# Fourier mixing folded over the positions, x2 stored before its scale, the context norm spread over gate b

## The chip, the cores and the metric

The kernel runs on one core of a Trainium2 chip. A core has five engines that work side by side: TensorE (PE, matrix products into the accumulators called PSUM), VectorE (DVE), ScalarE (ACT), GpSimd (POOL, here mostly an issuer of transfers) and SyncE (SP, an issuer of transfers). The metric is the device time of one execution in microseconds. The kernel before takes 2562.43 us, the median of 3 runs (2561.29 to 2563.51).

## The reference

Two transformer blocks stand one behind the other, over 1024 positions of 1024 channels: the first has sliding-window attention and a squared-ReLU MLP, then `rms_norm(h, final_norm)`; the second has a modulated norm, latent attention, a Fourier branch, two sigmoid gates and 16 experts. The change lies in the Fourier branch, in gate b, and where x enters the merge:

```python
def _fourier(f):                       # f: (B, T=1024, 512), in 4 groups of 128 channels
    fg = f.reshape(B, T, 4, 128).astype(jnp.float32)
    y = jnp.fft.fft2(fg, axes=(1, 3), norm="ortho").real
    return y.reshape(B, T, 512)

h  = _modulate(_rms(x, norm1_g), sh1, sc1);   hc = _modulate(_rms(ctx, norm1_g), csh1, csc1)
p  = h @ w_in
gb = sigmoid(p[..., OFF_GB:N_IN])
x  = x + g1 * ((ga * (attn_o @ w_o_attn) + gb * (_fourier(p[..., OFF_F:OFF_GA]) @ w_fourier)) @ w_out)
```

The real part of the two-dimensional transform is cos(positions) times cos(channels) minus sin(positions) times sin(channels). Cosine is even and sine odd about position 512, and each is again even or odd about 256; the change rests on this.

## The kernel before

Data lie channel by partition, 1024 positions along a row. Every product is done three times (`mm3`: high by high, low by high, high by low part of each operand), so every operand is split beforehand: ScalarE writes the high part (`make_hi` for weights, ACTIVATE Copy for data) and VectorE the rest (`make_lo`, a subtraction). Weights come through a ring of 3 raw buffers (SP issues their loads) and 4 places for split tiles; `tile(...)` numbers them in the order of use, and `done` says which product frees a place. PSUM has 8 banks of 512 columns; `next_banks` hands them out in rotation as the program is written, `claim` makes PE wait until the bank's last reader is through (`hand_over`). The order of the work on each engine is the order of the code, stage after stage: ..., MLP, final_*, four_*, gates_b_*, latent_*, heads_*, attention, merge_*, router_*, experts.

The stages that the change touches:
- final_*: the sums of squares (L1197), the two rows of factors spread over all partitions by a product with ones (L1205; row 0 for the second block's norm, row 1 for x's own scale in banks `f_rb1`), and U, the normed and modulated input, made tile k by tile k (DVE L1252, ACT L1218, DVE L1256).
- four_*: `f` = w_f times U for 4 groups (PE; groups 0 and 1 together as U's tiles come, 2 and 3 later), split into fT (ACT L1313, DVE L1335); the channel transform of each group, 8 blocks of 128 positions by 256 columns (cosine and sine) into Z (ACT L1317, DVE L1344); then the position transform: 16 tiles of a 2048 by 1024 table, each against 4 groups and both halves, into all 8 banks; then Y (ACT L1323, DVE L1351). In the middle, behind group 0's fT, DVE scales x into x2 (L1340, 8 instructions), and POOL stores it to memory (L1302); ACT's writing of Z over X waits for these stores.
- gates_b_*: for j = 0 to 7 gate b (48 products into 2 banks), a sigmoid (ACT L1458), w_fourier times Y (24 products), their product (DVE L1483) to memory. At j = 1 stands the context's norm as one piece: squares (ACT L269) and additions (DVE L275), sums (PE L283), root, diagonal, row (PE L310), and HC (DVE L1472 and L1475, ACT L1451).
- latent_*: among others the gate a products `ga_pe` and three rows of factors (L310).
- merge_*: POOL loads x2 (L2368), then gates and Fourier products (L2376, L2379); DVE makes M (L2403, L2407, L2409), PE multiplies by w_out, and DVE adds into X (L2416).

Of the kernel before, what the change touches and what calls it, by code (L numbers as in the profile page):

```python
# [102 lines left out]
def _program(nc, A, out, ctx):  # L103
# [1074 lines left out]
    fs_b, f_rb, f_rb1 = next_banks(), next_banks(2), next_banks(2)  # L1178
    fn.pe.plan(("sums",), ("row", 0), ("row", 1))
    fn.act.plan(("sd", 1), ("sd", 2), *[("hi", k) for k in range(8)])  # L1180
# [10 lines left out]
    def final_pe(pe):  # L1191
# [76 lines left out]
    f_b = {(g, i): next_banks(1, (f_rb, f_rb + 1, f_rb1, f_rb1 + 1)) for g in range(2) for i in range(2)}  # L1268
    z_b = {}
    for g in range(4):  # L1270
        if g > 1:
            for i in range(2):
                f_b[g, i] = next_banks(1, (f_rb1, f_rb1 + 1))
        for n in range(4):
            z_b[g, n] = next_banks(1, (f_rb1, f_rb1 + 1) if g == 0 else ())
    fo.act.plan(("cd",))
    fo.dve.plan(("cd",))
    for g in range(4):
        fo.act.plan(*[("f", g, i) for i in range(2)], *[("z", g, n) for n in range(4)])
# [4 lines left out]
    fo.pe.plan(("f", 0), ("f", 1), *[("z", 0, n) for n in range(4)], *[("z", 1, n) for n in range(4)])
    for g in (2, 3):
        fo.pe.plan(("f", g, 0), ("f", g, 1), *[("z", g, n) for n in range(4)])
    fo.pe.plan(*[("dft", c) for c in range(16)])
    fo.act.plan(*[("y", g, i) for g in range(4) for i in range(2)])
    fo.dve.plan(*[("y", g, i) for g in range(4) for i in range(2)])
    turn[0] = 0  # L1290
    T_F = [tile("w_f", g, fo.pe("f", g) if g < 2 else fo.pe("f", g, 1)) for g in range(4)]
# [12 lines left out]
    def four_act(act):
        act.wait_ge(*cd_in.at(1))
        act.e.activation(cd[0][:], cdr[:], ACT.Copy).then_inc(*fo.act.one("cd"))
        for g in range(4):
            make_hi(act, T_F[g if g > 1 else 0] + 3)
            for i in range(2):
                act.wait_ge(*f_mark(g, i))  # L1310
                if g:
                    act.wait_ge(*fo.pe("z", g - 1, 3))
                act.e.activation(fT[0][:, half(i)], bank(f_b[g, i]), ACT.Copy).then_inc(*fo.act.one("f", g, i))  # L1313
            for n in range(4):
                act.wait_ge(*fo.pe("z", g, n))
# [1672 lines left out]
```

## Time and profile before

| | |
|---|---|
| median of 3 runs | 2562.43 us |
| the profiled execution's own time | 2562.86 us |
| its span | 2561.0 us |
| mean granted clock of PE | 0.959 |
| PE busy | 2339.9 us (91%) |
| DVE busy | 1465.0 us (57%) |
| ACT busy | 1033.8 us (40%) |
| POOL busy | 271.4 us (11%) |
| memory traffic | 112 GB/s over the span |

The span is what the profile's records cover; 1.86 us of the execution lie around it. All times in rows are microseconds from the span's start. A busy PE is not a full PE: a product's record is longer (0.39 us) than the distance to the next one, and that distance is what counts.

### The profile page before, as it was taken

What the parts mean: (1) busy time and instruction counts of PE and PEld (TensorE: products, weight loads), DVE (VectorE), ACT (ScalarE), POOL (GpSimd) and SP (SyncE); (2) the same over time, 40 slices, a digit from 0 to 9 for tenths busy, and PEclk for the clock granted to TensorE, in tenths of its full rate; (3) what the DMA queues carried; (4) which work ended last, traced back from release to release, by engine and by line L of the source; (5) the groups of instructions that cost most, each with busy time, mean ns of one, the idle gap of its engine ahead of it and who ended that gap; (6) DMA issues with size and microseconds to landing.
All of it is one profiled execution on the core that took longest, in us unless ns stands there. A gap on an engine that the chain in (4) does not pass through costs nothing.

```text
span 2561.0 us, 28342 instructions
## 1 busy us (share of the span) xinstructions
PE 2339.9 (91%) x11580; PEld 1937.3 (76%) x11580; DVE 1465.0 (57%) x2132; ACT 1033.8 (40%) x1570; POOL 271.4 (11%) x360
## 2 busy tenths in 40 slices
PE   5999989999999999979999999899998988289997
PEld 3898768888888888758778878677777765268886
DVE  5677435454445445672232235867777543969997
ACT  3677324112212211432221123466666312258875
POOL 2111000011001111000000002700000100111211
PEclk9999999999999999989999999999999988689999
DMA  3124411243234333122222111100000621779996
GB/s 124 50 67 133 164 50 50 70 132 111 95 98 132 108 102 111 46 93 70 87 71 85 40 48 50 46 1 1 1 1 1 239 71 47 298 237 377 382 387 217
DMA packets 81026, 287.55 MB, mean 112 GB/s; under 512 B 10048, under 2 KB 10176, under 8 KB 79232
## 3 DMA queue, kind: packets, MB, share of 16 engines
q1 hardware_dynamic: 50256, 180.12, 19.6%
q0 software_dynamic: 29488, 101.43, 12.5%
q10 hardware_dynamic: 1152, 4.19, 0.4%
q8 instruction: 91, 1.49, 0.2%
q14 instruction: 39, 0.32, 0.0%
HBM read 250.05 MB, written 35.65 MB: 112 GB/s over the span
## 4 chain that ended last, share of the span: by engine, by line
PE 75%; DVE 14%; ACT 7%; DMA 1%; issue 1%; POOL 1%; POOLq 0%; DVEq 0%; ACTq 0%
PE psum L98 23%; PE psum L100 23%; PE psum L99 23%; DVE small L2268 4%; ACT PB L2204 3%; DVE MP_lo L2305 2%; ACT MP_hi L2234 1%; PE psum L868 1%; PE psum L841 1%; DVE idx L2545 1%; DVE vals L2543 1%; DVE cur L2548 1%; PE psum L310 1%; PE psum L2563 1%; DMA gal<-gas 1%
## 5 line engine op out<-in xcount | busy, mean ns | idle before, releaser
L98 PE MATMUL psum<-U_hi,w_hi 128*128 128x512 f32 (+1 forms) x1216 | 482.2, 397 | 20.7 <-DVE w_lo L231 9.3
L99 PE MATMUL psum<-U_lo,w_hi 128*128 128x512 f32 (+1 forms) x1216 | 479.1, 394 | 0.0
L100 PE MATMUL psum<-U_hi,w_lo 128*128 128x512 f32 (+1 forms) x1216 | 478.8, 394 | 0.0
L222 ACT ACTIVATE w_hi<-raw 128x1024 fp32r<-128x1024 f32 (+3 forms) x177 | 177.2, 1007 | 378.2 <-PE psum L100 370.0
L231 DVE TENSOR_TENSOR w_lo<-raw,w_hi 128x1024 fp32r<-128x1024 f32 (+3 forms) x177 | 206.2, 1172 | 190.4 <-ACT w_hi L222 190.1
L98 PEld LDWEIGHTS psum<-U_hi,w_hi 128*128 128x128 f32 (+1 forms) x1216 | 230.8, 190 | 74.2 <-issue 16.3
L100 PEld LDWEIGHTS psum<-U_hi,w_lo 128*128 128x128 f32 (+1 forms) x1216 | 230.0, 189 | 51.0 <-issue 0.8
L99 PEld LDWEIGHTS psum<-U_lo,w_hi 128*128 128x128 f32 (+1 forms) x1216 | 230.7, 190 | 48.1 <-issue 0.8
L98 PE MATMUL psum<-a_hi,w_hi 128*128 128x512 f32 x512 | 199.2, 389 | 0.0
L99 PE MATMUL psum<-a_lo,w_hi 128*128 128x512 f32 x512 | 199.2, 389 | 0.0
L100 PE MATMUL psum<-a_hi,w_lo 128*128 128x512 f32 x512 | 199.2, 389 | 0.0
L1058 DVE CUSTOM_DVE_ANT_0 mraw<-mraw,srow 128x512 f32<-128x512 f32 x128 | 85.8, 690 | 136.8 <-DMA mraw<-in_w_mod 130.2
L2305 DVE TENSOR_TENSOR MP_lo<-psum,MP_hi 128x512 fp32r<-128x512 f32 x160 | 109.6, 686 | 83.9 <-ACT MP_hi L2234 83.4
L1123 DVE TENSOR_TENSOR X<-psum,X 128x512 f32<-128x512 f32 x128 | 84.5, 688 | 96.6 <-PE psum L100 96.6
L1044 POOL DMA_DIRECT2D mraw<-in_w_mod x128 | 68.7, 537 | 657.7 <-DVE modb L1058 382.7
L231 DVE TENSOR_TENSOR w_lo<-rawe,w_hi 128x1024 fp32r<-128x1024 f32 x112 | 131.5, 1220 | 11.4 <-ACT w_hi L222 10.9
L1081 ACT ACTIVATE relu<-psum 128x512 f32<-128x512 f32 x64 | 38.2, 597 | 222.3 <-PE psum L100 217.5
L222 ACT ACTIVATE w_hi<-rawe 128x1024 fp32r<-128x1024 f32 x112 | 116.3, 1058 | 25.1 <-PE psum L100 25.1
L2140 PE MATMUL psum<-ident,PB 128*128 128x128 f32 x640 | 101.7, 282 | 23.4 <-DVE MP_lo L2305 22.2
L2140 PEld LDWEIGHTS psum<-ident,PB 128*128 128x128 f32 x640 | 75.7, 143 | 50.8 <-DVE MP_lo L2305 33.2
L2234 ACT ACTIVATE MP_hi<-psum 128x512 fp32r<-128x512 f32 x160 | 95.0, 594 | 42.5 <-PE psum L2140 41.5
L100 PEld LDWEIGHTS psum<-a_hi,w_lo 128*128 128x128 f32 x512 | 96.1, 188 | 20.0
(356 smaller groups left out, 4871.8 us busy)
## 6 DMA issues: line engine op xcount, KB each, us to landing
rawe<-in_w_e SPq DMA_DIRECT2D x112, 512.0 KB, 14.0
mraw<-in_w_mod POOLq DMA_DIRECT2D x128, 256.0 KB, 2.9
rawx<-in_w_e SPq DMA_DIRECT2D x56, 512.0 KB, 15.4
raw<-in_w_up SPq DMA_DIRECT2D x32, 512.0 KB, 3.6
raw<-in_w_dn SPq DMA_DIRECT2D x32, 512.0 KB, 3.6
raw<-in_w_e SPq DMA_DIRECT2D x24, 512.0 KB, 14.6
raw<-in_dft_t SPq DMA_DIRECT2D x16, 512.0 KB, 3.6
X<-in_xT SPq DMA_DIRECT2D x4, 1024.0 KB, 9.3
```

What stands on the lines that cost most here:

```text
L98: e.matmul(o, l[0], r[0], start=first, stop=False, skip_group_check=skip)
L99: e.matmul(o, l[0], r[1], start=False, stop=False, skip_group_check=skip)
L100: return e.matmul(o, l[1], r[0], start=False, stop=last, skip_group_check=skip)
L222: act.e.activation(w_hl[x.place][0][:, 0:x.width], w_raw[x.slot][:, 0:x.width], ACT.Copy).then_inc(w_hi, 1)
L231: dve.e.tensor_tensor(lo[:, 0:x.width], w_raw[x.slot][:, 0:x.width], f(hi[:, 0:x.width]), ALU.subtract).then_inc(w_lo, 1)
L1058: dve.e.tensor_tensor_reduce(mraw[n % 2][:], mraw[n % 2][:], srow[:, half(i % 2)], 1.0, 0.0, ALU.mult, ALU.add, dst).then_inc(*ml.dve.one( ...
L1123: dve.e.tensor_tensor(X[:, n, half(h)], bank(dn_b[i, n, h]), X[:, n, half(h)], ALU.add).then_inc(*ml.dve.one("x", i, n, h))
L2140: m = pe.e.transpose(bank(t_bank("turn", n), 256 * kb + P * i, 256 * kb + P * i + P), PB[(2 * u + i) % 5][:, (2 * t + kb) * P:(2 * t + kb ...
L2204: act.e.activation(PB[m % 5][:], s_of(m), ACT.Exp, bias=nmx[:, m % 8:m % 8 + 1], accum_out=msum(c)[:, z:z + 1]).then_inc(*at_s.act.one("ex ...
L2234: act.e.activation(MP[n % 4][0][:], bank(t_bank("turn", n)), ACT.Copy).then_inc(*at_s.act.one("turn", n))
L2268: dve.e.tensor_reduce(nmx[:, m % 8:m % 8 + 1], s_of(m), AX.X, ALU.max, negate=True).then_inc(*at_s.dve.one("max", m))
L2305: dve.e.tensor_tensor(lo[:], bank(t_bank("turn", n)), f(hi[:]), ALU.subtract).then_inc(*at_s.dve.one("turn", n))
```

## The change

The position transform is folded twice. After `f` (all 1024 positions of a group in two banks), ACT copies the second half out of PSUM (`second`), DVE forms the sums and differences f[n] +- f[1024-n], and then the same once more about 256 (`fold`); FF holds four quarters of 256 columns. The channel transform needs only cosine for the even half and only sine for the odd half, so its products are 128 columns wide (`over_channels`); one small float32 product with 3 columns gives what the fold leaves out (positions 256 and 512), and ACT's `alt` adds up the alternating sums for it. The position transform (`over_positions`) is 8 triples of products 256 columns wide for each group, with 2 table tiles in place of 16, and DVE unfolds its four parts into every second or fourth column of Y's row (`y`), some of them backwards. The groups run one after another in banks 4-5, 6-7, 2-3 and 0-1.

x is stored to memory without its scale as soon as the MLP has finished each tile; ACT copies the scale's row (`r1o`) and POOL stores it too. The 8 scaling instructions of DVE now stand in the merge (`x1`), behind a load of that row (`r1b`), which is issued ahead of the gates' loads. The context norm in gate b is spread: squares and additions at j = 1, sums at j = 2, row and HC at j = 4.

On PE, at the end of the channel transform and the start of the position transform, the rows before are (Z is stationary, w is a table tile):

```order
L99 MATMUL psum<-cd_lo,fT_hi 128x256
L100 MATMUL psum<-cd_hi,fT_lo 128x256
L98 MATMUL psum<-w_hi,Z_hi 128x512 [waits w_lo_made,fourier_dve]
L99 MATMUL psum<-w_lo,Z_hi 128x512
L100 MATMUL psum<-w_hi,Z_lo 128x512
```

After the change, at the end of group 0's position transform and the start of group 2's channel transform (L1486 is the 3-column product):

```order
L98 MATMUL psum<-w_hi,Z_hi 128x256
L99 MATMUL psum<-w_lo,Z_hi 128x256
L100 MATMUL psum<-w_hi,Z_lo 128x256
L1486 MATMUL psum<-small,cdr 128x3 [waits fourier_act,fourier_dve]
L98 MATMUL psum<-cd_hi,FF_hi 128x128 [waits fourier_dve]
L99 MATMUL psum<-cd_lo,FF_hi 128x128
L100 MATMUL psum<-cd_hi,FF_lo 128x128
```

One transform over 512 columns for all groups at the end has become a narrow one for each group, between the channel transforms.

On DVE, behind the last low part of U, before (cd is the channel table, X the scaling):

```order
L1330 TENSOR_TENSOR cd_lo<-cdr,cd_hi 128x256 [waits fourier_act]
L231 TENSOR_TENSOR w_lo<-raw_60,w_hi 128x1024 [waits w_hi_made]
L1335 TENSOR_TENSOR fT_lo<-psum,fT_hi 128x512 [waits fourier_act] x2
L1340 SCALAR_TENSOR_TENSOR X<-X,vec,psum 128x1024 [waits final_norm_products]
L1340 SCALAR_TENSOR_TENSOR X<-X,vec,psum 128x1024 x7
L1344 TENSOR_TENSOR Z_lo<-psum,Z_hi 128x512 [waits fourier_act] x4
```

and after, one `fold` (ff is the folded row; fe and fo the even and odd part):

```order
L1404 TENSOR_TENSOR ff_128<-psum,f2nd 128x1 [waits fourier_act]
L1405 TENSOR_TENSOR ff_128<-psum,f2nd 128x1
L1408 TENSOR_TENSOR fe<-psum,f2nd 128x511
L1409 TENSOR_TENSOR fo<-psum,f2nd 128x511
L1411 COPY small<-fe 128x1 [waits fourier_dve]
L1412 TENSOR_TENSOR ff_128<-fe 128x255
L1413 TENSOR_TENSOR ff_128<-fe 128x255
L1415 COPY ff_128<-fo 128x1 [waits fourier_dve]
L1416 TENSOR_TENSOR ff_128<-fo 128x255
L1417 TENSOR_TENSOR ff_128<-fo 128x255
```

The eight scalings have left this place, and ten short instructions for each group have come.

On POOL, at the start of the merge, the loads before are:

```order
L2368 DMA X<-x1s 128x2048 [waits x1_out0,attn_dve]
L2368 DMA X<-x1s 128x2048 [waits x1_out1]
L2368 DMA X<-x1s 128x2048 [waits x1_out2]
L2368 DMA X<-x1s 128x2048 [waits x1_out3]
L2376 DMA gal_202<-gas 128x1024 [waits ga_out2,ga_out0,ga_out3,ts_out1,ts_out0]
```

and after:

```order
L2520 DMA X<-x1s 128x2048 [waits x1_out0,attn_dve]
L2520 DMA X<-x1s 128x2048 [waits x1_out1]
L2520 DMA X<-x1s 128x2048 [waits x1_out2]
L2520 DMA X<-x1s 128x2048 [waits x1_out3]
L2522 DMA r1b<-r1s 128x1024 [waits r1_out]
L2530 DMA gal_215<-gas 128x1024 [waits ga_out2,ga_out0,ga_out3,ts_out1,ts_out0]
```

The row's load stands ahead of the first gate's.

```diff
@@ final norm @@
-    fs_b, f_rb, f_rb1 = next_banks(), next_banks(2), next_banks(2)
+    g_b = [4, 6, 2, 0]
+    fs_b, f_rb, f_rb1 = g_b[0], g_b[3], g_b[2]
+            if k == 3:
+                act.wait_ge(*fn.pe("row", 1))
+                act.e.activation(r1o[:], two(f_rb1), ACT.Copy).then_inc(*fn.act.one("r1o"))
@@ four_pool: x2 and the row of rsqrt to memory @@
+            pool.wait_ge(*ml.dve("x", 7, k, 1))
+            pool.e.dma_start(A["x1s"][:, k, :], X[:, k, :]).then_inc(x1_out[k // 2].sem, 16)
+        pool.wait_ge(*fn.act("r1o"))
+        pool.e.dma_start(A["r1s"], r1o[:]).then_inc(r1_out.sem, 16)
@@ four_act @@
+        def second(g):
+            act.wait_ge(*f_mark(g))
+            if g:
+                act.wait_ge(*fo.dve("fo", g - 1))
+            else:
+                act.wait_ge(*r1_out.at(1))
+            act.e.activation(f2nd[:], bank(g_b[g] + 1), ACT.Copy).then_inc(*fo.act.one("second", g))
+
+        def hi(g):
+            act.wait_ge(*fo.dve("fold", g))
+            if g > 1:
+                act.wait_ge(*fo.pe("chan", g - 2))
+            act.e.activation(FF[g % 2][0][:], ff[g % 2][:], ACT.Copy).then_inc(*fo.act.one("hi", g))
+            for s in range(2):
+                if g:
+                    act.wait_ge(*fo.act("alt", g - 1, s))
+                act.e.activation(alt[s][:], ff[g % 2][:, s:256:2], ACT.Copy, scale=(1.0, -1.0)[s],
+                                 accum_out=gx[:, 3 * g + 1 + s:3 * g + 2 + s]).then_inc(*fo.act.one("alt", g, s))
+
+        def one(g):
+            act.wait_ge(*fo.pe("e", g))
+            act.e.activation(ex[:, 3 * g:3 * g + 3], psum[:, g_b[g] + 1, 0:3], ACT.Copy,
+                             accum_out=y512[:, g:g + 1]).then_inc(*fo.act.one("e", g))
+
+        def z(g):
+            act.wait_ge(*fo.pe("chan", g))
+            if g > 1:
+                act.wait_ge(*fo.pe("pos", g - 2))
+            act.e.activation(Z[g % 2][0][:], two(g_b[g]), ACT.Copy).then_inc(*fo.act.one("z", g))
+
+        def second_p(g):
+            act.wait_ge(*fo.pe("pos", g))
+            if g:
+                act.wait_ge(*fo.dve("y", g - 1))
+            act.e.activation(p2nd[:], bank(g_b[g] + 1), ACT.Copy).then_inc(*fo.act.one("p2", g))
...
@@ four_dve @@
+        def fold(g):
+            x, a, b = ff[g % 2], bank(g_b[g]), f2nd
+            dve.wait_ge(*fo.act("second", g))
+            if g > 1:
+                dve.wait_ge(*fo.act("alt", g - 2, 1))
+                dve.wait_ge(*fo.dve("lo", g - 2))
+            e.tensor_tensor(x[:, 0:1], a[:, 0:1], b[:, 0:1], ALU.add)
+            e.tensor_tensor(x[:, 256:257], a[:, 0:1], b[:, 0:1], ALU.subtract)
+            if g:
+                dve.wait_ge(*fo.dve("fold", g - 1))
+            e.tensor_tensor(fe[:, 1:512], a[:, 1:512], b[:, 511:0:-1], ALU.add).then_inc(*fo.dve.one("fe", g))
+            e.tensor_tensor(fo_[:, 1:512], a[:, 1:512], b[:, 511:0:-1], ALU.subtract).then_inc(*fo.dve.one("fo", g))
+            dve.wait_ge(*fo.dve("fe", g))
+            e.tensor_copy(gx[:, 3 * g:3 * g + 1], fe[:, 256:257])
+            e.tensor_tensor(x[:, 1:256], fe[:, 1:256], fe[:, 511:256:-1], ALU.add)
+            e.tensor_tensor(x[:, 257:512], fe[:, 1:256], fe[:, 511:256:-1], ALU.subtract)
+            dve.wait_ge(*fo.dve("fo", g))
+            e.tensor_copy(x[:, 768:769], fo_[:, 256:257])
+            e.tensor_tensor(x[:, 513:768], fo_[:, 1:256], fo_[:, 511:256:-1], ALU.subtract)
+            e.tensor_tensor(x[:, 769:1024], fo_[:, 1:256], fo_[:, 511:256:-1], ALU.add).then_inc(
+                *fo.dve.one("fold", g))
...
+        def y(g):
+            a, b, x, E = bank(g_b[g]), p2nd, Yr[g % 2], ex[:, 3 * g:3 * g + 1]
+            dve.wait_ge(*fo.act("alt", 2 + g % 2, 1))
+            dve.wait_ge(*fo.dve("lo", 2 + g % 2))
+            if g > 1:
+                dve.wait_ge(*fo.dve("ylo", g - 2))
+            dve.wait_ge(*fo.act("e", g))
+            dve.wait_ge(*fo.act("p2", g))
+            e.tensor_copy(x[:, 512:513], y512[:, g:g + 1])
+            e.scalar_tensor_tensor(x[:, 0:512:4], a[:, 0:256:2], E, b[:, 0:256:2], ALU.add, ALU.subtract)
+            e.scalar_tensor_tensor(x[:, 1020:515:-4], a[:, 2:256:2], E, b[:, 2:256:2], ALU.add, ALU.add)
+            e.scalar_tensor_tensor(x[:, 2:512:4], a[:, 1:256:2], E, b[:, 1:256:2], ALU.subtract, ALU.subtract)
+            e.scalar_tensor_tensor(x[:, 1022:513:-4], a[:, 1:256:2], E, b[:, 1:256:2], ALU.subtract, ALU.add)
+            e.tensor_tensor(x[:, 1:512:2], a[:, 256:512], b[:, 256:512], ALU.subtract)
+            e.tensor_tensor(x[:, 1023:512:-2], a[:, 256:512], b[:, 256:512], ALU.add).then_inc(*fo.dve.one("y", g))
...
@@ four_pe (its 16 steps over the DFT tiles are gone) @@
-        for c in range(16):
-            w = use(pe, T_DFT[c])
-            for g in range(4):
-                l = [z[:, g, c % 8, 128 * (c // 8):128 * (c // 8) + 128] for z in (Zh, Zl)]
-                for i in range(2):
-                    m = mm3(pe.e, bank(2 * g + i), l, [x[:, half(i)] for x in w], c == 0, c == 15)
+        def over_channels(g):
+            x = FF[g % 2]
+            pe.wait_ge(*fo.dve("fold", g))
+            pe.wait_ge(*fo.act("alt", g, 1))
+            pe.e.matmul(psum[:, g_b[g] + 1, 0:3], cdr[:, 0:128], gx[:, 3 * g:3 * g + 3], start=True,
+                        stop=True).then_inc(*fo.pe.one("e", g))
+            pe.wait_ge(*fo.dve("cd"))
+            pe.wait_ge(*fo.dve("lo", g))
+            for n in range(8):
+                b, c, o = g_b[g] + n // 4, 128 * (n // 4), 128 * (n % 4)
+                if n == 4:
+                    pe.wait_ge(*fo.act("e", g))
+                m = mm3(pe.e, bank(b, o, o + 128), [y[:, n * P:n * P + P] for y in x], [y[:, c:c + 128] for y in cd],
+                        True, True)
+            m.then_inc(*fo.pe.one("chan", g))
+
+        def over_positions(g):
+            ws = [use(pe, t) for t in T_DFT]
+            pe.wait_ge(*fo.dve("z", g))
+            for n in range(8):
+                b, c, o = g_b[g] + n // 4, 256 * (n % 4), 256 * (n % 4 // 2)
+                m = mm3(pe.e, bank(b, o, o + 256), [y[:, n * P:n * P + P] for y in Z[g % 2]],
+                        [y[:, c:c + 256] for y in ws[n // 4]], n % 2 == 0, n % 2 == 1)
+            m.then_inc(*fo.pe.one("pos", g))
...
+        project(2)
+        over_channels(0)
+        over_channels(1)
+        project(3)
+        over_positions(0)
+        over_channels(2)
+        over_positions(1)
+        over_channels(3)
+        over_positions(2)
+        over_positions(3)
@@ gates_b_pe @@
-            if j == 1:
+            if j == 2:
                 nc_.sums(pe)
+            if j == 4:
                 nc_.rows(pe, cdg)
@@ merge @@
+        def x1(n):
+            dve.wait_ge(*x1_in[n // 2].at(1))
+            dve.wait_ge(*r1_in.at(1))
+            dve.e.scalar_tensor_tensor(X[:, n, :], X[:, n, :], GF[:, n:n + 1], r1b[:], ALU.mult, ALU.mult).then_inc(
+                *mg.dve.one("x1", n))
+        pool.wait_ge(*r1_out.at(1))
+        pool.e.dma_start(r1b[:], A["r1s"]).then_inc(r1_in.sem, 16)
```

In the last stages only the numbers of banks and of weight buffers shift: the rotation of banks leaves gate b at bank 6 in place of bank 2.

## Rows read from the trace of the kernel before

**Rows 1.** The page's chain that ended last: shares of the span by engine.
```profile
PE 75%; DVE 14%; ACT 7%; DMA 1%; issue 1%; POOL 1%; POOLq 0%; DVEq 0%; ACTq 0%
```
**Rows 2.** Timeline of PE, Fourier, gate b: start, duration, instruction, [idle before <-releaser].
```profile
1126.16 0.36 PE L98 MATMUL psum<-cd_hi,fT_hi 128*128 128x256 f32 x1 [1.50 <-DVE fT_lo L1335]
...
1139.19 0.58 PE L98 MATMUL psum<-cd_hi,fT_hi 128*128 128x256 f32 x1 [9.92 <-DVE fT_lo L1335]
...
1173.71 0.47 PE L98 MATMUL psum<-w_hi,Z_hi 128*128 128x512 f32 x1 [1.46 <-DVE Z_lo L1344]
...
1262.52 0.47 PE L98 MATMUL psum<-U_hi,w_hi 128*128 128x512 f32 x1 [1.50 <-DVE Y_lo L1351]
...
1405.33 0.39 PE L98 MATMUL psum<-U_hi,w_hi 128*128 128x512 f32 x1
```
**Rows 3.** Windows: stretch, length, busy (count) PE, PEld, DVE, ACT, POOL, clock, DMA.
```profile
100.00:160.00 60.00, 60.00 (x410) 54.25 (x409) 41.35 (x129) 42.29 (x121) 5.34 (x10) 1.00 0.21 63
...
1174.00:1261.00 87.00, 87.00 (x384) 71.70 (x382) 18.94 (x16) 15.47 (x15) 0.00 (x0) 1.00 0.29 88
```
**Rows 4.** Timeline of PE: neighbours of 128 and of 256 columns.
```profile
103.71 0.28 PE L98 MATMUL psum<-PT_hi,vz_hi 128*128 128x128 f32 x1
103.83 0.28 PE L99 MATMUL psum<-PT_lo,vz_hi 128*128 128x128 f32 x1
...
1155.33 0.28 PE L98 MATMUL psum<-cd_hi,fT_hi 128*128 128x256 f32 x1
1155.45 0.28 PE L99 MATMUL psum<-cd_lo,fT_hi 128*128 128x256 f32 x1
```
**Rows 5.** Timeline of PE: the context norm's sums and row in gate b.
```profile
1285.66 1.01 PE L283 MATMUL psum<-vec,csq 128*128 128x1 f32 x4 [6.56 <-DVE csq L275]
1287.68 1.22 PE L310 MATMUL psum<-cdg,ones 128*128 128x256 f32 x2 [1.01 <-DVE cdg L302]
```
**Rows 6.** Timeline of DVE: short and long instructions.
```profile
1085.35 0.17 DVE L1227 TENSOR_TENSOR mod<-mod,vec 128x16 f32<-128x16 f32 x1
...
1118.78 0.41 DVE L1330 TENSOR_TENSOR cd_lo<-cdr,cd_hi 128x256 fp32r<-128x256 f32 x1
1119.11 1.22 DVE L231 TENSOR_TENSOR w_lo<-raw,w_hi 128x1024 fp32r<-128x1024 f32 x1
1125.33 1.29 DVE L1335 TENSOR_TENSOR fT_lo<-psum,fT_hi 128x512 fp32r<-128x512 f32 x2 [5.00 <-ACT fT_hi L1313]
1126.53 9.61 DVE L1340 SCALAR_TENSOR_TENSOR X<-X,vec,psum 128x1024 f32<-128x1024 f32 x8
...
1290.00 0.48 DVE L1475 SCALAR_TENSOR_TENSOR HC_lo<-ctmp,mod,HC_hi 128x256 fp32r<-128x256 f32 x1 [0.58 <-ACT HC_hi L1451]
1290.40 0.48 DVE L1472 SCALAR_TENSOR_TENSOR ctmp<-cT,mod,psum 128x256 f32<-128x256 f32 x1
```
**Rows 7.** Timeline of ACT: copies, and a sigmoid in the latent stage.
```profile
1106.34 1.15 ACT L1218 ACTIVATE U_hi<-tmp,mod 128x1024 fp32r<-128x1024 f32 x1 [1.36 <-DVE tmp L1252]
...
1510.31 0.60 ACT L1623 ACTIVATE gas<-psum 128x512 f32<-128x512 f32 x1 [4.84 <-PE psum L100]
```
**Rows 8.** Groups of ACT by shape: count, busy, mean ns, idle before.
```profile
L676 ACT ACTIVATION_READ_ACCUMULATOR EX<-EX,small 128x1 f32 x128 | 24.1, 189 | 0.0
...
L676 ACT ACTIVATE EX<-EX,small 128x128 f32<-128x128 f32 x16 | 6.2, 389 | 1.0 <-DVE small L773 1.0
```
**Rows 9.** Waits of PE: in the latent stage, and in the merge (total, times, longest).
```profile
PE psum L98 <- ACT st L292: 0.4, 1, 0.4
...
PE psum L98 <- DVE M_lo L2409: 10.0, 3, 5.0
```
**Rows 10.** Merge: timeline of DVE, a window, and DVE behind a w_out product.
```profile
2016.73 1.29 DVE L2403 TENSOR_TENSOR mtm<-psum,gal 128x512 f32<-128x512 f32 x2 [10.43 <-DMA gal<-gas]
...
2000.00:2020.00 20.00, 20.00 (x81) 16.30 (x81) 3.49 (x5) 1.32 (x2) 3.96 (x8) 0.91 0.96 373
...
2091.22 0.75 DVE L2416 SCALAR_TENSOR_TENSOR X<-psum,mod,X 128x512 f32<-128x512 f32 x1 [4.62 <-PE psum L100]
```

More of the change, by code:

```diff
@@ L1284, in _program @@
[L1284 to L1291, printed above, removed]
@@ L1354, in four_pe @@
-    def four_pe(pe):
+        make_hi(act, T_F[3])
+        second(0)
+        second(1)
+        hi(0)
+        hi(1)
+        make_hi(act, T_DFT[1])
+        second(2)
+        one(0)
+        z(0)
+        one(1)
+        hi(2)
+        z(1)
+        make_hi(act, T_DFT[1] + 1)
+        second(3)
+        second_p(0)
+        one(2)
+        hi(3)
+        z(2)
+        y_hi(0)
+        second_p(1)
+        one(3)
+        z(3)
+        y_hi(1)
+        second_p(2)
+        make_hi(act, T_DFT[1] + 2)
@@ new lines, in four_act, with four_dve, lo, z_lo @@
+        y_hi(2)
+        second_p(3)
+        y_hi(3)
+    def four_dve(dve):
+        e = dve.e
+        def fold(g):
[19 more added lines that the diff above has]
+                *fo.dve.one("fold", g))
+        def lo(g):
+            dve.wait_ge(*fo.act("hi", g))
+            e.tensor_tensor(FF[g % 2][1][:], ff[g % 2][:], f(FF[g % 2][0][:]), ALU.subtract).then_inc(
+                *fo.dve.one("lo", g))
+        def z_lo(g):
+            dve.wait_ge(*fo.act("z", g))
+            e.tensor_tensor(Z[g % 2][1][:], two(g_b[g]), f(Z[g % 2][0][:]), ALU.subtract).then_inc(
+                *fo.dve.one("z", g))
+        def y(g):
[13 more added lines that the diff above has]
+            e.tensor_tensor(x[:, 1023:512:-2], a[:, 256:512], b[:, 256:512], ALU.add).then_inc(*fo.dve.one("y", g))
+        def y_lo(g):
+            dve.wait_ge(*fo.act("yhi", g))
+            e.tensor_tensor(Y[1][:, g, :], Yr[g % 2][:], f(Y[0][:, g, :]), ALU.subtract).then_inc(
+                *fo.dve.one("ylo", g))
+        make_lo(dve, T_F[3])
+        dve.wait_ge(*fo.act("cd"))
+        e.tensor_tensor(cd[1][:], cdr[:], f(cd[0][:]), ALU.subtract).then_inc(*fo.dve.one("cd"))
+        dve.wait_ge(*fn.dve("lo", 7))
+        for i in range(2):
+            e.memset(ff[i][:, 512:513], 0.0).then_inc(*fo.dve.one("zero", i))
+        fold(0)
+        fold(1)
+        lo(0)
+        lo(1)
+        make_lo(dve, T_DFT[1])
+        z_lo(0)
+        fold(2)
+        z_lo(1)
+        lo(2)
+        fold(3)
+        lo(3)
+        y(0)
+        z_lo(2)
+        y_lo(0)
+        make_lo(dve, T_DFT[1] + 1)
+        y(1)
+        z_lo(3)
+        y_lo(1)
+        make_lo(dve, T_DFT[1] + 2)
+        y(2)
+        y_lo(2)
+        y(3)
+        y_lo(3)
@@ L1355, in four_pe @@
         ws = [use(pe, T_F[g]) for g in range(2)]
         for g in range(2):
-            for i in range(2):
-                claim(pe, f_b[g, i])
+            claim(pe, g_b[g], 2)
         for k in range(8):
@@ L1466, in gates_b_dve @@
                     nc_.add(dve, k)
+            make_lo(dve, T_FO[j] + 3)
+            for i in range(2):
+                dve.wait_ge(*gb.pe("fo", j, i))
+                dve.wait_ge(*gb.act("gb", j, i))
+                if j > 1:
+                    dve.wait_ge(*ts_out[j % 2].at(j // 2))
+                dve.e.tensor_tensor(tsb[j % 2][:, half(i)], bank(fo_b[j, i]), gbs[j % 2][:, half(i)],
+                                    ALU.mult).then_inc(*gb.dve.one("fo", j, i))
+            if j == 2:
                 nc_.diag(dve, cdg)
+            if j == 4:
                 dve.wait_ge(*gb.pe("nc", "row"))
```

221 lines of the change are left out of this document (93 added, 128 removed).

## The prediction, made before the changed kernel was run

> **What bounds the kernel now.** I read the page's chain first: PE holds 75% of what ended last [rows 1], so a product that disappears shortens the run wherever PE has no wait beside it. Then the timeline of PE between the end of the MLP and the latent stage. The Fourier part begins, after the products of groups 0 and 1, at 1126.16 - 1.50 = 1124.66 and ends where gate b's first product starts, at 1262.52; gate b ends at 1405.33 [rows 2]. That is 137.9 us and 142.8 us. In the first stretch PE waits four times, 1.50, 9.92, 1.46 and 1.50 us, together 14.4, always for the low part that VectorE makes; the long one is the time of eight scalings of X, 9.61 us, that stand ahead on VectorE [rows 2, 6]. The position transform is 87.0 us without a gap: 384 products, 0.2266 us from one to the next [rows 3]. So PE alone bounds this stage, but for the waits.
>
> **The change part by part.** The sums go by distances between neighbours, not by the durations of the records. The steps of PE in the Fourier part, from 1124.66:
>
> Products of w_f for groups 2 and 3: 2 x 48 x 0.2266 = 21.8 us, as before.
>
> Channel transform: 96 products of 256 columns become 96 of 128. Neighbours of 256 columns are 0.12 us apart, and neighbours of 128 columns of the same three-product form are 0.12 too [rows 4]: half the columns buy nothing. 96 x 0.12 = 11.5 us before and after. New are four float32 products of 3 columns. The nearest row is the four records of the context's sums, 1.01 us for two products [rows 5]; so 0.4 us each, between 0.2 and 0.8: +1.6 us.
>
> The Trainium skill, "TensorE: Matmul & The Clock Gate", section "Back-to-back issue gap", gives about 81 ns for each product of 128 columns in a stream of weight loads and products. The rows of this case disagree, 120 ns; by the page the 96 products would take 7.8 us and the whole would be 3.7 us shorter. I go by the rows.
>
> Position transform: 384 products of 512 columns become 4 x 24 = 96 of 256: 96 x 0.12 = 11.5 in place of 87.0 us.
>
> So PE has 21.8 + 11.5 + 1.6 + 11.5 = 46.4 us of work. Does it have to wait? I laid the three engines' orders side by side with these prices. VectorE: a one-column instruction at most 0.17, 511 columns 0.60 (1.29 for two, of which the second's record ends 0.09 after the next start), 255 columns 0.33 (1118.78 to 1119.11), 256 columns of the three-operand form 0.40 (1290.00 to 1290.40), 1024 columns 1.20 [rows 6]. An estimate for 128 columns of that form: 0.40 less 128 times (1.20 - 0.40)/768 us is 0.27. So `fold` is 4 x 0.17 + 2 x 0.60 + 4 x 0.33 = 3.2 us, `y` is 0.17 + 4 x 0.27 + 2 x 0.40 = 2.1 us. ScalarE: 1024 columns at most 1.15, 512 columns 0.60, a sum over 128 columns 0.39 + 0.19 = 0.6 [rows 7, 8].
>
> PE: group 2's projection to 1135.6, channels 0 and 1 to 1142.2 (PE is at each of them later than `lo`, which ends near 1133 and 1134), projection of group 3 to 1153.1, positions 0 to 1156.0, channels 2 to 1159.3, positions 1 to 1162.2, channels 3 to 1165.5, positions 2 to 1168.4. The late chain is VectorE's, from group 3's `f` at 1153.1: copy 0.6, fold 3.2, ScalarE's high part 1.15, lo 1.2, y of group 0 2.1, Z's low part 1.2, Y's 1.2, a weight tile 1.2, y of group 1 2.1, Z's low part of group 3 1.2, and 0.5 for hand-offs: 1168.8. Positions 3 can start at 1168.8, 0.4 us late. ScalarE's copy of the small product stands behind other work too, and may cost 0.1 to 0.2 us in each group: 0.5 in all. Positions 3 end at 1168.8 + 2.9 + 0.4 = 1172.1. Y's last low part comes near 1180, and is first wanted after 48 products of gate b, at 1183. Gate b thus starts at 1172.1 in place of 1262.52: **-90.4 us**. Of this 75.5 are products, 14.4 waits less 0.9 new ones, 3.2 the slower products behind the 9.92 us wait (the first takes 0.58 where others take 0.28 [rows 2, 4]), less 1.6 small products. What covers the fold is PE's own work; each microsecond by which fold and twice y are dearer comes out at positions 3.
>
> Storing x: the eight stores go to a time when VectorE and PE do not wait for transfers. The row's copy on ScalarE, about 1.1 us, falls into a pause of 1.36 us between two high parts [rows 7]. Both 0; without this cover 1.1. Fourteen table tiles less are 14 splits less on engines that wait here: 0.
>
> Gate b: 8 x 72 products at 0.2266 are 130.5 us, the stage takes 142.8: the context norm costs 12.3 now. After the change PE still does the sums and the row, 1.01 and 1.22 us at the slow level, about 1.1 together at the full one [rows 5]. New is a wait: the sums go to bank 4, which the last product of j = 1 has just filled, so PE waits for VectorE's 512 columns, 0.69 and a hand-off, 0.9 us; everything of j = 2 is queued behind it. Squares, additions and HC lie beside 16.3 us of products in each j, and the last of the eight HC steps, some 12 us after PE's start of j = 5, comes before bank 5 is claimed 13.6 us after it. **-10.3 us**, between -12.3 and -9.
>
> Latent stage: the shifted rotation puts the row of factors (L310) into banks that gate a's sigmoid has yet to read. 0.60 us and hand-offs, 0.9; a wait of 0.4 on the same rotation goes [rows 7, 9]: **+0.5 us**.
>
> Merge: its start hangs on a transfer. VectorE waits 10.43 us for the first gate's data, which land with 4.2 MB of X ahead of them, at 373 GB/s [rows 10]. The row adds 0.52 MB ahead: 1.4 us. Behind it VectorE's chain for M is what PE waits for at the end, 10.0 us [rows 9], so the shift goes through: **+1.4 us**, from 0 if the transfers overlap otherwise to 3. The scalings, 8 x 1.2 = 9.6 us, stand where VectorE waits 4.62 us for each w_out product [rows 10], and hide.
>
> Sum: 2562.86 - 90.4 - 10.3 + 0.5 + 1.4 = 2464.1 for an execution like the profiled one; the median is 0.4 lower, 2463.7. I take 2463.5.
>
> **The rivals.**
>
> *Forecast*, 2458 to 2468: 66%.
>
> *Short and reversed columns are dear on VectorE.* No row shows a backward row, or a result written into every fourth column. If these took twice the time for each column, fold would be 2.1 us dearer (2 x 511 + 4 x 255 columns at 1.04 ns) and y 1.1: the late chain grows by 2.1 + 2 x 1.1 = 4.3, and the earlier folds stay covered. 2468; with the fixed part doubled too, some 2475. Nothing in the trace speaks for it but that the form is absent. 12%.
>
> *The clock falls.* If the many short products with waits between them let PE drop to 1.2 GHz, the 24.6 us of channel and position products take up to twice that: 2464 + 24.6 = 2488. Against it: in 100 to 160 us PE runs 410 records, many of 128 and 256 columns, at a granted clock of 1.00 [rows 3]. The Trainium skill, "TensorE: Matmul & The Clock Gate", section "A second HAM failure mode: psum-queue depth-cycling", describes such drops from small pauses; by that rule this rival is the outcome, and this case's stretch does not bear it out. 4%.
>
> *The merge pays.* If the first scaling holds up VectorE's emptying of PSUM, or the row lands after all the gates' data, another 3 to 5 us: 2468. For it: this is where transfers are densest. Against: 4.62 us of room. 7%.
>
> *The norm in gate b is not spread.* If a bank or a buffer makes PE wait at j = 2 or 4 as long as at j = 1 now, 10 us stay: 2474. 4%.
>
> *Better*: no row price in the merge, no late chain, products of 128 columns nearer the page: 2455 to 2458. 6%.
>
> *Slower than before.* One mechanism: 72 short instructions on VectorE (4 x 10 and 4 x 7, and the splits) in series with PE. It needs 2567.5 - 2463.5 = 104 us more, 1.4 us more for each; the rows have 0.17 to 0.6. It would decide only from there. 1%.
>
> **How the numbers follow.** The likeliest is 2463.5. 2457 to 2474 takes in the forecast, most of the first rival, the merge's, and the norm's; outside stay the clock, the extremes and a part of the first, under 2 in 10. A difference of 0.2%, 5 us, is what can be told from none here; every case but the last is beyond it.
>
> **What would show it.** In the changed profile: position products 0.12 us apart, 96 of them; channel products not closer than 0.11; gate b's first product near 1172; a PE wait under 1 us ahead of the last position products; no clock under 1.00 between 1125 and 1280; a wait near 0.9 us at the sums of j = 2; gates' first data some 1.4 us later behind the last attention step. Wrong it would be with a fold over 4 us, with a wait over 3 us in the Fourier part, or with VectorE behind PE in the w_out products.

## The result, and the profile after

The changed kernel takes 2462.07 us (median of 4, 2458.78 to 2465.36), the kernel before 2562.22 us (median of 4) beside it: ratio 0.9609, 95% interval 0.9592 to 0.9625. The profiled execution took 2458.78 us, its span 2456.9 us, against 2562.86 and 2561.0. The forecast was 2463.5.

The chain that ended last, as the profile's page gives it; most of it is still PE's [rows 1]:

```profile
PE 74%; DVE 15%; ACT 7%; DMA 2%; issue 1%; POOL 0%; POOLq 0%; DVEq 0%; ACTq 0%
```

The timeline of PE in the changed kernel: the first product of w_f, the small product and its neighbours, channel and position products, gate b's first product, the context norm's sums and row, the latent stage's first product.

```profile
1103.54 0.47 PE L98 MATMUL psum<-U_hi,w_hi 128*128 128x512 f32 x1 [1.65 <-DVE U_lo L1262]
...
1136.27 0.28 PE L1486 MATMUL psum<-small,cdr 128*128 128x3 f32 x2
1136.41 0.31 PE L98 MATMUL psum<-cd_hi,FF_hi 128*128 128x128 f32 x1
...
1139.12 0.33 PE L1486 MATMUL psum<-small,cdr 128*128 128x3 f32 x2
...
1164.52 0.33 PE L98 MATMUL psum<-w_hi,Z_hi 128*128 128x256 f32 x1
...
1167.45 0.28 PE L98 MATMUL psum<-w_hi,Z_hi 128*128 128x256 f32 x1
...
1170.32 0.40 PE L98 MATMUL psum<-U_hi,w_hi 128*128 128x512 f32 x1
...
1203.94 0.61 PE L283 MATMUL psum<-vec,csq 128*128 128x1 f32 x4 [0.78 <-DVE tsb L1616]
...
1237.17 0.59 PE L310 MATMUL psum<-cdg,ones 128*128 128x256 f32 x2
...
1302.93 0.39 PE L98 MATMUL psum<-U_hi,w_hi 128*128 128x512 f32 x1
```

Read the distances. From w_f's first product to gate b's it is 66.78 us, 159.90 before (1262.52 [rows 2] less 1102.62). Gate b takes 132.61 us in place of 142.81. 24 channel products take 2.71 us (1136.41 to 1139.12), 0.113 each; the last 48 position products 5.80 us (1164.52 to 1170.32), 0.121 each; a pair of small products 0.14 (1136.27 to 1136.41).

PE's waits between 1120 and 1420 us (line, releaser: total, times, longest), all of them:

```profile
PE psum L1703 <- ACT sqk L1696: 3.3, 2, 1.7
PE psum L283 <- DVE tsb L1616: 0.8, 1, 0.8
PE psum L310 <- ACT gas L1769: 0.7, 1, 0.7
PE psum L1822 <- ACT kpT L1847: 0.6, 1, 0.6
```

None lies in the Fourier part, where PE waited 14.4 us. The 0.8 is at the context sums; the 0.7 is the one in the latent stage that the shifted rotation of banks brings; the other two stood there before.

The clock, in the same columns as [rows 3], is full in the Fourier part, and in the windows behind it as far as the end of gate b too (1.00 from 1175 to 1303):

```profile
1125.00:1175.00 50.00, 50.00 (x320) 45.32 (x319) 35.35 (x82) 22.27 (x47) 0.00 (x0) 1.00 0.10 33
```

VectorE's timeline there: the first and the last row of group 0's fold, the start of group 1's, one y, and the last low part of Z.

```profile
1126.22 0.16 DVE L1404 TENSOR_TENSOR ff<-psum,f2nd 128x1 f32<-128x1 f32 x1 [4.89 <-ACT f2nd L1327]
...
1126.36 0.68 DVE L1408 TENSOR_TENSOR fe<-psum,f2nd 128x511 f32<-128x511 f32 x1
1126.96 0.68 DVE L1409 TENSOR_TENSOR fo<-psum,f2nd 128x511 f32<-128x511 f32 x1
...
1129.01 0.15 DVE L1404 TENSOR_TENSOR ff<-psum,f2nd 128x1 f32<-128x1 f32 x1
...
1164.28 0.14 DVE L1438 COPY ff<-small 128x1 f32<-128x1 f32 x1
1164.35 0.44 DVE L1439 SCALAR_TENSOR_TENSOR ff<-psum,small,p2nd 128x128 f32<-128x128 f32 x1
1164.62 0.43 DVE L1440 SCALAR_TENSOR_TENSOR ff<-psum,small,p2nd 128x127 f32<-128x127 f32 x1
...
1166.08 1.22 DVE L1427 TENSOR_TENSOR Z_lo<-psum,Z_hi 128x1024 fp32r<-128x1024 f32 x1
```

A fold takes 2.79 us (1126.22 to 1129.01), a y 1.80 (1164.28 to 1166.08). Backward rows and results in every fourth column cost no more than straight ones: 0.60 us for 511 columns, as for 512 straight ones before, and 0.27 for 128, which is the estimate that the prediction made from straight rows. The last low part of Z ends at 1167.30, and PE starts on it at 1167.45.

The merge, to be held against [rows 10] and [rows 9]: POOL's load of x and VectorE's first product with a gate and its first sum, then PE's waits for M. (gal is a loaded tile of gate a, tsl one of the stored products of gate b.)

```profile
1893.15 2.17 POOL L2520 DMA_DIRECT2D X<-x1s  x4 [342.93 <-DVE oT_lo L2428]
...
1911.48 1.29 DVE L2563 TENSOR_TENSOR mtm<-psum,gal 128x512 f32<-128x512 f32 x2 [10.98 <-DMA gal<-gas]
1913.57 1.23 DVE L2567 TENSOR_TENSOR mtm<-mtm,tsl 128x1024 f32<-128x1024 f32 x1 [0.80 <-DMA tsl<-ts]
```

```profile
PE psum L98 <- DVE M_lo L2569: 10.4, 3, 5.0
```

The two rows of VectorE stand 18.33 and 20.42 us behind the first load; before it was 17.95 and 19.27 (1998.78 to 2016.73 and 2018.05), so the sum comes 1.15 us later. The landings of the loads, counted from the start of the first load of x, show where it comes from. Before, the last piece of x landed after 16.6 us, gal after 17.9, tsl after 19.1; now the last piece of x after 15.7, the row after 17.0, gal after 18.2, tsl after 20.3. The row thus takes 1.3 us. Two shifts that nobody forecast stand beside it: x lands 0.9 us earlier, and tsl comes 2.1 us behind gal where it was 1.3. They nearly cancel. From PE's first product of w_o_attn to its last wait for M it is 63.18 us, 62.04 before.

By stages the profiled execution's 104.1 us are: start of the Fourier part 0.9 later, Fourier part -93.1, gate b -10.2, latent stage -1.1, heads -0.4, attention -1.7, merge to M +1.1, the rest +0.4. The later start is not the change's price: with the same code up to there it lay between 1102.66 and 1104.40 in the profiled runs of the experiments, and at 1102.61 in the kernel before with the storing alone.

### The profile page after: what moved, and what is told of

It is laid out like the page before. It is cut to its first block, busy times and chain, and to the rows that moved or that the text cites. A ratio compares the mean times of both kernels' runs of the same rounds, so it can differ in the third digit from the quotient of the medians.

```text
span 2456.9 us, 27784 instructions
## 1 busy us (share of the span) xinstructions
PE 2254.2 (92%) x11300; PEld 1868.5 (76%) x11300; DVE 1458.6 (59%) x2168; ACT 1021.6 (42%) x1569; POOL 273.3 (11%) x362
## 4 chain that ended last, share of the span: by engine, by line
PE 74%; DVE 15%; ACT 7%; DMA 2%; issue 1%; POOL 0%; POOLq 0%; DVEq 0%; ACTq 0%
PE psum L98 23%; PE psum L99 23%; PE psum L100 22%; DVE small L2414 4%; ACT PB L2350 3%; DVE MP_lo L2451 2%; ACT MP_hi L2380 1%; PE psum L868 1%; PE psum L841 1%; DVE idx L2709 1%; DVE vals L2707 1%; DVE cur L2712 1%; DMA tsl<-ts 1%; DVE w_lo L231 1%; PE psum L2727 1%
## 5 line engine op out<-in xcount | busy, mean ns | idle before, releaser
L222 ACT ACTIVATE w_hi<-raw 128x1024 fp32r<-128x1024 f32 (+2 forms) x163 | 162.1, 1001 | 304.7 <-PE psum L100 296.9
L231 DVE TENSOR_TENSOR w_lo<-raw,w_hi 128x1024 fp32r<-128x1024 f32 (+2 forms) x163 | 188.9, 1167 | 114.3 <-ACT w_hi L222 113.9
```

The source lines that it names most:

```text
L222: act.e.activation(w_hl[x.place][0][:, 0:x.width], w_raw[x.slot][:, 0:x.width], ACT.Copy).then_inc(w_hi, 1)
L231: dve.e.tensor_tensor(lo[:, 0:x.width], w_raw[x.slot][:, 0:x.width], f(hi[:, 0:x.width]), ALU.subtract).then_inc(w_lo, 1)
```

## Experiments

All are held against runs of the kernel before on the same chip (medians of 2562.1 to 2563.0 us in their groups). The edits are shown in short, with lines joined and parts left out. Each trace is of one execution. Below, "Fourier part" is the distance from w_f's first product to gate b's, "gate b" from there to the latent stage's first, "attention" from its first transpose to the first product of w_o_attn, "chain for M" from there to the start of the product behind PE's last wait for M.

**The changed kernel again.**

> The changed kernel once more, on the chip and in the rounds of the other runs of this group, as the measure for them: its first four times lay between 2458.8 and 2465.4, growing with a falling mean granted clock (0.963, 0.963, 0.961, 0.960). Theory (the scatter is the length of the half-clock stretches, not the transfers): times between 2455 and 2465, the higher ones at the lower clock. Rival: the first four were high as a group and the kernel's usual time is 2455, which would make the run with the late row (2454.9) no gain.

2460.70 us (2456.76 to 2464.00, 5 runs), ratio 0.9602 (0.9589 to 0.9616). The rival falls: the usual time is not 2455. The scatter is there again, with the longest time at the lowest mean clock (0.962) and the shortest at the highest (0.965). The two profiled executions differ by 2.0 us (2458.78 and 2460.78), and attention alone by more, 342.33 us in the first and 346.22 in this one. The windows at its two ends, in the first profile and then in this one:

```profile
1550.00:1572.00 22.00, 15.12 (x66) 11.55 (x67) 10.33 (x11) 9.65 (x15) 0.23 (x1) 0.84 0.00 1
1868.00:1892.00 24.00, 15.84 (x115) 13.39 (x113) 16.41 (x24) 14.05 (x24) 0.00 (x0) 1.00 0.00 1
```

```profile
1550.00:1572.00 22.00, 17.32 (x65) 12.79 (x66) 8.64 (x9) 8.75 (x13) 0.00 (x0) 0.69 0.00 1
1868.00:1892.00 24.00, 18.86 (x118) 16.70 (x118) 15.64 (x22) 13.48 (x23) 0.00 (x0) 0.86 0.00 1
```

The granted clock is 0.84 and 1.00 in one, 0.69 and 0.86 in the other, with the same code. Times alone therefore don't settle 1 or 2 us here; the distances of the trace do.

**The norm in one piece.**

```
-            if j == 2: nc_.sums(pe)
-            if j == 4: nc_.rows(pe, cdg)
+            if j == 1: nc_.sums(pe); nc_.rows(pe, cdg)     # ACT's and DVE's part moved to j = 1 too
```

> The changed kernel with the context norm back in one piece at j = 1. Theory (the norm's 10 us were an exposed chain): gate b, from its first product to the latent stage's first, takes 142.8 us again in place of 132.6, with the wait of 6.6 us ahead of the sums, the 1.0 ahead of the row and the half-clock products behind them; the time is 10 us above the changed kernel's. Rival (most of the 10 us came from the clock or from elsewhere): the stage takes under 137 us. The latent stage loses its new wait of 0.7 us ahead of the row only if the rotation of banks returns; the norm claims the same number of banks, so it stays.

2469.69 us (2469.45 to 2470.93, 4 runs), 9.0 above the changed kernel's 2460.70, where 10 was expected. Gate b is 141.94 us long, and the old waits are back:

```profile
PE psum L283 <- DVE csq L275: 6.6, 1, 6.6
...
PE psum L310 <- DVE cdg L302: 1.0, 1, 1.0
```

```profile
1190.00:1210.00 20.00, 14.69 (x55) 12.11 (x56) 10.48 (x24) 8.62 (x17) 0.00 (x0) 0.74 0.06 23
```

The norm's chain was exposed, and it costs the half-clock products behind it too: behind the row, products of 512 columns stand 0.43 us apart for a while, then 0.23. How long varies: the short distance is back 5.5 us after the first product behind the row in the kernel before, after 3.7 us here, after 2.5 us in the next run. From the row to the end of the stage it is accordingly 117.65, 116.84 and 116.25 us, with the same waits ahead. So the term is 8.8 to 10.2 us.

**Only the storing.** The kernel before, with `x1` taken out of `four_dve` and put into `merge_dve`, and with `r1o`, `r1s` and `r1b` as in the change.

> The kernel before with one part of the change alone: x2 stored unscaled, its scale applied in the merge. Theory: PE's wait of 9.92 us ahead of group 1's channel transform shrinks to about 2 us (copy 0.6, low part 1.3 and hand-offs), as the eight scalings of 9.61 us leave VectorE there; the half-clock products behind it, 3.2 us, become full-speed ones; the merge costs 1.2 us more. In all 10 us below the kernel before, 2552. Rival (the scalings only hid another wait, such as the store of x that must be done before Z overwrites X): the wait stays over 6 us and the time is within 5 us of the kernel before. With this run the fold's own share of the 100 us is what is left: about 79 us.

2554.79 us (7 runs, 2549.88 to 2557.10), ratio 0.9968 (0.9956 to 0.9979): 7.7 us below the kernel before in its group, where 10 was expected; the interval reaches from 5 to 11. The trace is clearer. The Fourier part takes 150.07 us in place of 159.90; PE's row behind the wait, which was 9.92:

```profile
1131.23 0.39 PE L98 MATMUL psum<-cd_hi,fT_hi 128*128 128x256 f32 x1 [2.01 <-DVE fT_lo L1340]
```

The chain for M takes 63.44 us (+1.4): the row pushes gal's landing from 17.9 to 19.3 us behind the first load of x. Of the 93.1 us, 9.8 are thus the storing's when it is put on the kernel before, and the other 83.3 come with the fold. No run has the fold without the storing, so that the two parts simply add up is not shown from the other side.

**The row's load behind the gates' first.**

```
-        pool.wait_ge(*r1_out.at(1)); pool.e.dma_start(r1b[:], A["r1s"])   # ahead of the gates
+            if j == 1: pool.wait_ge(*r1_out.at(1)); pool.e.dma_start(r1b[:], A["r1s"])
```

> The changed kernel with the load of the scale's row moved from ahead of the gates' loads to behind the first four of them. Theory (transfers land in the order of their issue, at some 400 GB/s): VectorE's chain for M starts 1.2 us earlier, counted from the first load of X: the first product with a gate after 17.9 us in place of 18.3 and the first sum after 19.3 in place of 20.4; the last product of w_out moves with it; the time falls by 1.2 us, less than the runs scatter. Rival (the transfers share the bandwidth and end together): no shift in the trace.

2454.93 us (2454.64 to 2456.76, 4 runs). In the trace the chain for M takes 61.14 us in place of 63.18. The first product with a gate stands 17.06 us behind the first load (17.9 expected), the first sum 18.38 (19.3 expected), without a wait for tsl:

```profile
1911.02 1.29 DVE L2564 TENSOR_TENSOR mtm<-psum,gal 128x512 f32<-128x512 f32 x2 [9.79 <-PE psum L100]
```

The view names PE as the releaser, but the transfer was the later one: gal landed at 1910.92, 0.1 us ahead of this row. The row's place costs 2.0 us, where I expected 1.2, and the landings split them: gal comes 16.97 us behind the first load of x in place of 18.24, which is the 1.3 us of the row; the other 0.8 is the stretched distance between gal and tsl, 2.1 us in the changed kernel and 1.27 here, where the next gal has it instead. What causes that stretch is not shown. The two profiled executions with the short attention, this one (342.20 us, 2456.76) and the first of the changed kernel (342.33 us, 2458.78), lie 2.0 us apart, as their chains do. The medians differ by more, 5.8 us; that the move itself shortens attention is not shown, and why all four runs were short stays open.

**The gates' loads ahead of x's.**

```
-        for i in range(4): pool.e.dma_start(X[:, 2 * i:2 * i + 2, :], ...)       # ahead of the gates
+            if 0 < j < 5: i = j - 1; pool.e.dma_start(X[:, 2 * i:2 * i + 2, :], ...)  # behind tsl j
+            if j == 5: pool.e.dma_start(r1b[:], A["r1s"])
```

> The changed kernel with the loads of x in the merge (4 x 1 MB) and of the row issued behind the first gates' loads, one piece behind each of the pairs j = 1 to 4, the row behind j = 5. Theory (M's chain hangs on the gates' data, which stand behind 4.7 MB, and PE waits for the chain at its end): the first product with a gate starts about 8 us after PE's first product of w_o_attn ends its bank instead of waiting 11 us; the chain of 8 x 5.4 us then ends about 10.5 us earlier; PE's three waits of 1.1, 5.0 and 4.3 us shrink to under 1 us together and the half-clock products behind them go; 10 to 12 us less, 2451. Rival (the transfers of x then collide with the later gates' loads and the weights): the chain's period grows over 5.4 us, waits for gal or tsl appear on VectorE, and under 5 us are gained.

2447.77 us (2447.44 to 2448.05, 4 runs), ratio 0.9555 (0.9539 to 0.9571); 12.9 below the changed kernel's 2460.70, a little more than the 10 to 12 expected. VectorE's first two products with a gate, and PE's wait for M:

```profile
1901.51 0.68 DVE L2565 TENSOR_TENSOR mtm<-psum,gal 128x512 f32<-128x512 f32 x1
1904.33 0.69 DVE L2565 TENSOR_TENSOR mtm<-psum,gal 128x512 f32<-128x512 f32 x1 [2.13 <-PE psum L100]
```

```profile
PE psum L98 <- DVE M_lo L2571: 1.2, 1, 1.2
```

The first starts without a wait, 6.1 us behind the first load (1895.43), and the second waits for PE, no longer for a transfer. The chain for M takes 52.50 us in place of 63.18, the w_out products behind it 85.86 in place of 87.77. The rival's collision doesn't come, though the DMA engines are full:

```profile
1917.00:1937.00 20.00, 20.00 (x90) 16.53 (x90) 15.38 (x18) 7.19 (x8) 5.26 (x10) 1.00 1.02 410
```

VectorE's period is 5.44 us (M's low parts at 1907.41, 1912.85, 1918.29) with no wait for gal or tsl.

**The banks mended.**

```
-            if j == 2: nc_.sums(pe)                  # ahead of the gate products
+                if j == 2 and i == 0: nc_.sums(pe)   # behind the first of them
+    turn[0] = 2                                      # ahead of the latent stage
```

> The changed kernel with two things mended in the order of banks: the context sums stand behind the first gate product of j = 2, when bank 4 has been read, and the rotation is set back to bank 2 after gate b. Theory: the wait of 0.78 us ahead of the sums goes and gate b takes 131.8 us in place of 132.6; the wait of 0.73 us ahead of the latent stage's row goes, and the one of 0.4 that the kernel before had may come back. 1 us less in all, below what the times can tell; the stages of the trace decide. Rival (other waits take their place): gate b stays at 132.6.

2459.88 us (2457.74 to 2461.32, 4 runs): by the time nothing. By the trace gate b takes 131.57 us in place of 132.60, and the row in the latent stage waits no longer; the old short wait stands there again:

```profile
PE psum L98 <- ACT st L292: 0.4, 1, 0.4
```

**A probe on VectorE's late chain.**

```
         y(1)
+        for i in range(2): e.tensor_copy(probe[i][:], f(U[0][:, i, :]))
         z_lo(3)
```

> The changed kernel with two more instructions of 1024 columns on VectorE between y of group 1 and the last low part of Z; their result is not used. Theory (VectorE's late chain ends as PE comes to the last position products: the last low part of Z ends at 1167.30, the products start at 1167.45): the two cost 1.1 us each, PE waits about 2 us ahead of the last 24 position products, and gate b's first product comes 68.9 us after the first product of w_f in place of 66.8. Rival (the chain has slack that the trace hides): no wait, 66.8 us.

2461.73 us (2461.11 to 2465.03, 4 runs). The two copies took 1.2 us together, not 2.2:

```profile
1166.87 1.28 DVE L1475 COPY probe<-U_hi 128x1024 f32<-128x1024 f32 x2
...
1168.07 1.21 DVE L1428 TENSOR_TENSOR Z_lo<-psum,Z_hi 128x1024 fp32r<-128x1024 f32 x1
```

```profile
1169.33 0.39 PE L98 MATMUL psum<-w_hi,Z_hi 128*128 128x256 f32 x1 [0.92 <-DVE Z_lo L1428]
```

The Fourier part took 68.00 us, 1.2 more: all that was added came out, 0.92 as a wait and 0.28 around it (the record of the product ahead of a wait reaches 0.16 us past the place where the next one would start, and the first product behind it takes 0.23 us in place of 0.12). Counted from w_f's first product, the last position products start 1.1 us later for 1.2 us added, so the cover is 0.1 us. The price of the probe was mis-sized, the place where VectorE binds was not.

**A probe on the merge's scalings.**

```
             if n < 7: x1(n + 1)
+            for i in range(3): dve.e.tensor_tensor(probe[i][:], r1b[:], r1b[:], ALU.add)
```

> The changed kernel with three more instructions of 1024 columns on VectorE in each of the eight steps of the w_out products, behind the scaling; their result is not used. Theory (the scalings are hidden: of 10.88 us in each step VectorE is idle 5.9, 4.69 ahead of the first half and 1.20 ahead of the second): 3 x 1.2 = 3.6 us more in each step still fit, the w_out products take 87 to 88 us as before and the time stays within 2455 to 2465. Rival (VectorE's order makes PE or the weight's low part wait, as 3.6 us is more than the 1.2 ahead of the second half): PE waits appear in the w_out products, 2 us and more in each of seven steps, 2475 or above.

2464.87 us (2458.73 to 2465.97, 4 runs). PE's waits from the chain for M to the end of the w_out products, and the one at the norm's sums, which was 3.28:

```profile
PE psum L98 <- DVE M_lo L2571: 10.4, 3, 5.0
PE psum L283 <- DVE sq L275: 5.5, 1, 5.5
PE psum L98 <- DVE w_lo L231: 0.4, 1, 0.4
```

The wait of 0.4 us stands at 1918.90, in the chain for M and ahead of the probe's instructions; the kernel before with the storing alone has one like it. In the w_out products PE waits nowhere: seven steps swallow 3.4 us of extra work each. Only the last step's has no cover, and the wait at the sums grows by 2.2 us. From M to the sums it is 90.90 us in place of 87.31; 1.4 of these 3.6 us have no wait beside them, and what they are is open (without the wait at the sums this stretch took 83.9 to 84.7 us in the other profiles with the fold and x loaded first, 85.4 in the kernel before with the storing alone, and 85.4 here). The change's own scalings stand in steps 0 to 6 and ahead of step 0, so they don't meet this.

**Both mended.** The gates' loads first, and the banks.

> The changed kernel with both: the gates' loads ahead of x's in the merge, and the banks mended. Theory: the gains add up, as they lie in stages apart: 1 us below the run with the gates first alone (2447.8), 2446.5 to 2447.5; it is the fastest of all. Rival (the set-back rotation brings a wait in the later stages, whose banks shift too): slower than 2448.

2446.73 us (2444.88 to 2453.57, 5 runs), ratio 0.9555 (0.9540 to 0.9570). Gate b 131.57 us, chain for M 51.89. Four of the five runs lie below 2448, one at 2453.57. It beats both kernels, by 14.0 and 116 us; from the run with the gates first alone no time tells it apart.

## Why the prediction was right, and where its terms were off

*Fourier part, -90.4 forecast, -93.1 measured.* The mechanism held: 75 us of products, four waits gone, full clock. The position products take 11.6 us in place of 87. The 2.7 us are three terms that I priced too high. The small products: 0.14 to 0.19 us in each group, not 0.4, together 1.0 us. Channel products of 128 columns: 0.113 us apart, not 0.12, 0.7 us; the row read for it shows a single pair, and its neighbours from 103.60 to 104.05 stand 0.113 apart as well. Waits: none, where I had put 0.9 (VectorE's fold took 2.79 us, not 3.2, y 1.80, not 2.1, and ScalarE's copy of the small product cost PE nothing). One attribution was off: of the 3.2 us of slower products that the prediction puts behind the 9.92 us wait, about 2.0 stand there (24 products from 1139.19 to 1144.09 take 4.90 us, where 24 at 0.12 take 2.9); the rest is spread over the stage. That half the columns buy next to nothing held: 0.113 against 0.12 us. The Trainium skill, "TensorE: Matmul & The Clock Gate", section "Back-to-back issue gap", has 81 ns for products of 128 columns; 24 in a row took 2.71 us here at full clock, so for this three-product form the measurement stands against it.

*The late chain binds at the last position products.* Forecast 0.4 us late, measured just on time, and the probe showed that there is 0.1 us to spare. The chain was 1.4 us shorter than forecast (1153.02 to 1167.30), and PE came some 1 us earlier than forecast; that the two met again within 0.2 us is luck, that this is the place where they meet is not. The rival of dear short and reversed columns needed this place and found it; what was wrong with it was its price.

*Storing x.* 9.8 us of the Fourier part (the run with the storing alone), near the 9.61 us of the scalings: 7.9 us of the wait, and about 2 of slower products behind it. The scalings are hidden in the merge, as forecast.

*Gate b, -10.3 forecast, -10.2 measured*, with the wait of 0.78 us at the sums (forecast 0.9). The run with the norm whole gives 9.3 for the same term; the difference is the length of the half-clock stretch.

*Latent stage, +0.5 forecast, -1.1 measured.* The waits moved as forecast (0.73 us for ScalarE's gas is new, forecast 0.9; 0.45 for st is gone). The stage, up to its row of factors, was shorter all the same, and it varies between 101.7 and 106.8 us over the runs with the fold, with the clock: the granted clock from 1302 to 1406 was 0.95 in the run with the shortest and 0.90 in the one with the longest. The prediction counted such changes in no stage behind gate b.

*Merge, +1.4 forecast, +1.1 measured.* The rule "what is ahead in the queue comes first" held: the row shifts gal's landing by 1.3 us. That the sum came out at 1.1 is partly luck, as x landed 0.9 us earlier and tsl 0.8 us later than the row explains.

*Attention*, which the prediction left out, gave 1.7 us in the profiled execution and can take 2 back: 342.2 to 346.3 us over the runs with the fold. The profiled execution, forecast at 2464.1, took 2458.8. Of the 5.3 us, 2.7 are the Fourier part's, 1.6 the latent stage's and 1.7 attention's, the other stages take 0.7 back. That the medians, 2462.1 and 2460.7, lie nearer to the 2463.5 is in part luck: in the second profile attention was 2.1 us longer than before the change, and covered most of what the Fourier part gave beyond the forecast.

*The rivals.* The clock did not fall, short and reversed columns were not dear, the norm stayed spread, and the merge did not pay more; each by the rows above.

## What to carry to other kernels

When a stage waits for an elementwise chain at its end, look at what the chain's first instruction waited for: here 4.7 MB of loads, wanted some 50 us later, stood ahead of the 2 MB wanted at once, and their order was worth 10.7 us in the chain, where the change's own row, 0.5 MB, cost 1.3. A short serial chain (the norm) costs its length and then the half-clock products behind it; spread over a stage that has room, it costs little more than its products (here one wait of 0.78 us). Where a stage's times scatter by more than the effect, compare distances between the same two instructions.

## What the runs showed of the hardware

A copy on VectorE from SBUF to SBUF took 0.60 us for 1024 float32 columns, half of the 1.2 us that a subtraction with two inputs takes [rows 6]. The Trainium skill, "VectorE: DVE Perf Modes", section "Mode 2×_2P — use both read ports for one tensor", states such a doubling for instructions with one source in SBUF; the trace agrees. Reading backwards and writing into every second or fourth column cost VectorE nothing: 511 reversed columns 0.60 us, 256 columns written two apart 0.34 us, 128 columns written four apart 0.27 us. A float32 product of 3 columns, two records, takes PE 0.14 to 0.19 us between neighbours. In one queue of POOL the merge's loads landed in the order of their issue, 1.3 us apart for each 0.5 MB where nothing else came between, at about 400 GB/s.
